# Own places for the gate weights of the fourth expert pair, and another order at the end of the routing

## What is computed

```python
gp = jax.nn.softmax(x @ w_group_router + b_group_router); g_val, g_idx = lax.top_k(gp, 1)
el_sel = (x @ w_expert_router + b_expert_router) # the 8 experts of that group
e_val, e_idx = lax.top_k(jax.nn.softmax(el_sel), 2); e_val = e_val / e_val.sum()
combine = one_hot(g_idx * 8 + e_idx) * (g_val * e_val)
for e in range(32):
    hdn = jax.nn.silu(x @ w_gate[e]) * (x @ w_up[e])        # 1024 -> 256
    y = y + combine[:, e:e + 1] * (hdn @ w_down[e])         # 256 -> 1024
```

## Time and profile before

| | us |
|---|---|
| median of 3 runs | 614.64 (614.0 to 615.8) |
| the profiled execution | 614.34 |
| its span | 612.7 |
| TensorE busy | 532.0 (87%) |
| VectorE busy | 218.6 (36%) |
| ScalarE busy | 169.6 (28%) |
| GpSimd busy | 139.4 (23%) |
| all transfers | 140.80 MB, mean 230 GB/s |

### The profile page before, as it was taken

How to read it: one execution, slowest core, us unless ns; L and a number is a source line. 1 busy time by engine, 2 the same in 40 slices (tenths; PEclk the granted TensorE clock), 3 DMA queues, 4 the chain that set the end, 5 groups by cost and what they waited for, 6 DMA issues and landing times.

```text
span 612.7 us, 9450 instructions
## 1 busy us (share of the span) xinstructions
PE 532.0 (87%) x3252; PEld 391.5 (64%) x3253; DVE 218.6 (36%) x602; ACT 169.6 (28%) x421; POOL 139.4 (23%) x230
## 2 busy tenths in 40 slices
PE   4899999999989999999956976899938779999984
PEld 4788988987558668888854633566624555556651
DVE  4753244333667755347671121111101111121111
ACT  6833343332443332135431111111111111111110
POOL 0132232222503200015525012122201122222212
PEclk9999999999999999999966999999959989999998
DMA  8741000012313101299894299999999999999993
GB/s 315 294 108 36 13 23 1 24 46 76 116 57 104 34 35 36 60 409 420 317 355 190 95 318 376 371 374 395 378 375 404 372 382 387 375 358 370 383 339 71
DMA packets 33445, 140.80 MB, mean 230 GB/s; under 512 B 10488, under 2 KB 11147, under 8 KB 21350
## 3 DMA queue, kind: packets, MB, share of 16 engines
q1 hardware_dynamic: 25776, 124.33, 52.4%
q0 software_dynamic: 5856, 12.60, 8.5%
q10 hardware_dynamic: 1766, 3.25, 1.6%
HBM read 131.15 MB, written 16.46 MB: 241 GB/s over the span
## 4 chain that ended last, share of the span: by engine, by line
DMA 26%; PE 22%; DVE 4%; issue 3%; ACT 1%; POOL 1%; DVEq 0%; POOLq 0%; ACTq 0%; SPq 0%
PE ps L847 11%; DMA expert_w<-in_w_gate 11%; DMA expert_w<-in_w_up 9%; PE ps L863 5%; DMA token_gates<-gate_rows 2%; DMA more_rows<-token_rows,idx_now 2%; DMA g_rows<-token_rows,idx_all 1%; DMA token_rows<-h_sb 1%; PE ps L506 1%; PE ps L507 1%; PE ps L511 1%; PE ps L765 1%; DVE xT L1490 1%; PE ps L834 1%; ACT s_act L1134 1%
## 5 line engine op out<-in xcount | busy, mean ns | idle before, releaser
L847 PE MATMUL ps<-expert_w,xT 128*64 128x256 f32 x1152 | 134.1, 390 | 12.9 <-issue 5.1
L847 PEld LDWEIGHTS ps<-expert_w,xT 128*64 128x64 f32 x1152 | 98.6, 141 | 52.1 <-issue 22.2
L863 PE MATMUL ps<-expert_w,hT 128*64 128x512 f32 x272 | 63.9, 611 | 18.0 <-DVE hT L1508 16.8
L1664 POOL DMA_INDIRECT out<-y_sb,idx_now x17 | 27.2, 1602 | 175.9 <-issue 128.2
L1501 DVE SCALAR_TENSOR_TENSOR hid<-s_act,gate,ps 128x256 f32<-128x256 f32 x18 | 12.0, 666 | 139.5 <-ACT s_act L1134 139.5
L863 PEld LDWEIGHTS ps<-expert_w,hT 128*64 128x64 f32 x272 | 21.9, 140 | 49.2 <-issue 42.9
L1134 ACT ACTIVATE s_act<-ps,gate 128x256 f32<-128x256 f32 x18 | 8.5, 474 | 131.2 <-PE ps L847 131.2
L506 PE MATMUL ps<-w_in_hi,aT_hi 128*128 128x384 f32 (+2 forms) x120 | 43.7, 369 | 0.0
L507 PE MATMUL ps<-w_in_lo,aT_hi 128*128 128x384 f32 (+2 forms) x120 | 40.8, 345 | 0.0
L1513 DVE COPY y_sb<-ps 128x512 f32<-128x512 f32 x18 | 12.4, 692 | 74.1 <-PE ps L863 68.4
L1139 ACT ACTIVATE y_sb<-ps 128x512 f32<-128x512 f32 x18 | 10.8, 597 | 78.8 <-PE ps L863 73.2
(11 more groups left out here) (227 smaller groups left out, 924.6 us busy)
## 6 DMA issues: line engine op xcount, KB each, us to landing
expert_w<-in_w_gate SPq DMA_DIRECT2D x32, 1024.0 KB, 9.2
expert_w<-in_w_up SPq DMA_DIRECT2D x32, 1024.0 KB, 9.5
expert_w<-in_w_down SPq DMA_DIRECT2D x30, 1024.0 KB, 9.5
w_in_raw<-in_w_in SPq DMA_DIRECT2D x8, 608.0 KB, 10.4
w_out_raw<-in_w_out SPq DMA_DIRECT2D x8, 512.0 KB, 3.8
token_rows<-h_sb ACTq DMA_DIRECT2D x6, 512.0 KB, 8.3
out<-h_sb SPq DMA_DIRECT2D x6, 512.0 KB, 11.5
x_sb<-in_x_prompt SPq DMA_DIRECT2D x4, 512.0 KB, 12.7
```

The source lines that it names most:

```text
L847: mm = pe.matmul(ps[r, GU_BANK[q.o], g * FH:(g + 1) * FH], xT[:, q.o, k, r], w_gu(b, lane, k, g), start=(k == 0), stop=(k == KD - 1))
L863: mm = pe.matmul(ps[r, 4 + half, :], hT[:, q.o, k, r], w_dn(b, lane, k, half), start=(k == 0), stop=(k == 1))
L1664: pool.indirect_dma_start(out=out, out_offset=bass.IndirectOffsetOnAxis(ap=idx, axis=0), in_=y_sb[:, buf, :], in_offset=None, compute_op=A ...
```

## The change

- The gate parts of pair 3 get places of their own, w_gate3_0 behind w2 and w_gate3_1 at the end of the third region. To make room, `more_rows` becomes the fourth buffer of y_sb, which the surplus pass uses for its results.
- SyncE loads parts 0 to 3 of pair 2, waits for the first gather, loads parts 4 and 5, then waits for the surplus slot products, the stored token weights and all indices, and loads the gate parts of pair 3. The refill of pair 3 then has only the up and down parts.
- The loops of all engines write out pairs 0 to 3 and 13 to 15 and run three turns over pairs 4 to 12.
- TensorE's order at the end of the routing becomes: logits of tile 5 (first half), transposes, slots(1), ranks(4), slots(2), slots(3), logits (second half), slots(4), more_slots(1) to (3), ranks(5), the token column of slots(5) alone, the two other columns of slots(5), the count product, more_slots(4), more_slots(5).
- VectorE computes the weight factors of tile 5 after the token indices of the first gather instead of ahead of `slot_of`.

Nothing is put into TensorE's pauses beyond this work.

```diff
-        (qT, w_in_raw, aT_hi, cT_kv, q_x, w_in_lo, o_hi, o_lo, w_out_hi_o, w_out_lo_o, w2) = region(
+        (qT, w_in_raw, aT_hi, cT_kv, q_x, w_in_lo, o_hi, o_lo, w_out_hi_o, w_out_lo_o, w2, w_gate3_0) = region(
-            [("expert_w2", [P, 2, 3, 2 * D], F32)], pick="under_")
+            [("expert_w2", [P, 2, 3, 2 * D], F32), ("w_gate3_0", [P, 2 * D], F32)], pick="under_")
...
-            [("g_rows", [P, 3, D], F32), ("more_rows", [P, D], F32), ("xT", [P, 2, KD, P], F32), ("y_sb", [P, 4, D], F32),
-             ("s_act", [P, 2, FH], F32), ("hid", [P, 2, 2, P], F32), ("hT", [P, 2, 2, P], F32), ("more_gate", [P, PAIRS, 2], F32)],
+            [("g_rows", [P, 3, D], F32), ("xT", [P, 2, KD, P], F32), ("y_sb", [P, 4, D], F32),
+             ("s_act", [P, 2, FH], F32), ("hid", [P, 2, 2, P], F32), ("hT", [P, 2, 2, P], F32), ("more_gate", [P, PAIRS, 2], F32),
+             ("w_gate3_1", [P, 2 * D], F32)],
             pick="under_")
         weights = (w0, w1, w2)
+        w_gate3 = (w_gate3_0, w_gate3_1)
+        more_rows = y_sb[:, 3, :]
...
-        def w_gu(b, lane, k, g):
-
+        def w_gu(j, b, lane, k, g):
+            if isinstance(j, int) and j == 3 and g == 0:
+                return w_gate3[lane][:, k * FH:(k + 1) * FH]
             return weights[b][:, lane, g, k * FH:(k + 1) * FH]
...
-                sp.dma_start(weights[b][:, lane, what, :], src).then_inc(part_in[n], 16)
+                first = isinstance(j, int) and j == 3 and what == 0
+                sp.dma_start(w_gate3[lane][:, :] if first else weights[b][:, lane, what, :], src).then_inc(part_in[n], 16)
...
-            for b in range(3):
-                pair(b, 0, b, False)
-            with eng.Fori(1, PAIRS // 3) as i:
-                for b in range(3):
-                    pair(3 * i + b, i, b, False)
-            pair(PAIRS - 1, PAIRS // 3, 0, True)
+            for j in range(4):
+                pair(j, j // 3, j % 3, False)
+            with eng.Fori(1, 4) as i:
+                for b in range(1, 4):
+                    pair(3 * i + b, i + b // 3, b % 3, False)
+            for j in range(PAIRS - 3, PAIRS):
+                pair(j, j // 3, j % 3, j == PAIRS - 1)
...
-            load_pair(sp, 2, 2)
+            load_pair(sp, 2, 2, range(4))
+            sp.wait_ge(main.gathered[0], 16)
+            load_pair(sp, 2, 2, range(4, 6))
+            sp.wait_ge(more_mm, NT)
+            sp.wait_ge(gates_stored, 16 * NT)
+            sp.wait_ge(idx_done, 13)
+            load_pair(sp, 3, 0, range(2))
...
-                used(lambda q: q.g_mm)
-                load_pair(sp, j, b, range(2))
+                if not (isinstance(j, int) and j == 3):
+                    used(lambda q: q.g_mm)
+                    load_pair(sp, j, b, range(2))
                 used(lambda q: q.gu_mm)
                 load_pair(sp, j, b, range(2, 4))
                 used(lambda q: q.y_mm)
-                if isinstance(j, int):
+                if isinstance(j, int) and j == PAIRS - 1:
                     load_last_down(j, b)
                 else:
                     load_pair(sp, j, b, range(4, 6))
 
-            with sp.Fori(1, PAIRS // 3) as i:
-                for b in range(3):
-                    refill(3 * i + b, b)
-            refill(PAIRS - 1, 0)
+            refill(3, 0)
+            with sp.Fori(1, 4) as i:
+                for b in range(1, 4):
+                    refill(3 * i + b, b % 3)
+            for j in range(PAIRS - 3, PAIRS):
+                refill(j, j % 3)
...
+            def slot_product(i, at, block, cols, last):
+
+                for c in range(2):
+                    mm = pe.matmul(ps[:, 5, at + cols.start * E:at + cols.stop * E], slot_a[:, i % SLOT_BUFS, 2 * block + c, :],
+                                   slot_b[:, i % SLOT_BUFS, c, cols, :].rearrange("t n e -> t (n e)"),
+                                   start=(i == 0 and block == 0 and c == 0), stop=(last and c == 1), skip_group_check=True)
+                return mm
+
             def slots(i):
 
                 pe.wait_ge(slot_a_done, 2 * i + 1)
                 pe.wait_ge(slot_b_done, 2 * (i + 1))
-                for c in range(2):
-                    mm = pe.matmul(ps[:, 5, 0:3 * E], slot_a[:, i % SLOT_BUFS, c, :], slot_b[:, i % SLOT_BUFS, c, :, :].rearrange("t n e -> t (n e)"),
-                                   start=(i == 0 and c == 0), stop=(i == NT - 1 and c == 1), skip_group_check=True)
-                mm.then_inc(slot_mm, 1)
+                slot_product(i, 0, 0, slice(0, 3), False).then_inc(slot_mm, 1)
+
+            def last_slots():
+
+                pe.wait_ge(slot_a_done, 2 * NT - 1)
+                pe.wait_ge(slot_b_done, 2 * NT - 1)
+                slot_product(NT - 1, 0, 0, slice(0, 1), False).then_inc(slot_mm, 1)
+                pe.wait_ge(idx_done, 2)
+                pe.wait_ge(slot_b_done, 2 * NT)
+                slot_product(NT - 1, 0, 0, slice(1, 3), True).then_inc(slot_mm, 1)
 
             def more_slots(i):
 
                 pe.wait_ge(slot_a_done, 2 * (i + 1))
-                if i == 1:
-                    pe.wait_ge(idx_done, 5)
-                for c in range(2):
-                    mm = pe.matmul(ps[:, 5, 128:128 + 3 * E], slot_a[:, i % SLOT_BUFS, 2 + c, :], slot_b[:, i % SLOT_BUFS, c, :, :].rearrange("t n e -> t (n e)"),
-                                   start=False, stop=(i == NT - 1 and c == 1), skip_group_check=True)
-                mm.then_inc(more_mm, 1)
+                slot_product(i, 128, 1, slice(0, 3), i == NT - 1).then_inc(more_mm, 1)
...
             h_transposes(last, 1)
+            slots(1)
+            ranks(last - 1)
+            slots(2)
+            slots(3)
             logits(last, 1)
-            ranks(last - 1)
-            for i in range(1, last):
-                slots(i)
+            slots(last - 1)
+            for i in range(1, last - 1):
+                more_slots(i)
             ranks(last)
-            slots(last)
+            last_slots()
             pe.wait_ge(pos_done, NT)
             pe.matmul(ps[:, 6, 128:128 + E], ones_bf, m_sum[:, 0, :], start=True, stop=True).then_inc(total_mm, 1)
-            for i in range(1, NT):
-                more_slots(i)
+            pe.wait_ge(idx_done, 5)
+            more_slots(last - 1)
+            more_slots(last)
...
             route_experts(NT - 1)
-            route_weights(NT - 1)
             slot_of(NT - 1)
             dve.wait_ge(slot_mm, NT)
 
@@ -1457,7 +1485,9 @@
                                     ).then_inc(idx_done, 1)
 
             slot_tokens(0, idx_all)
+            route_weights(NT - 1)
             table_place(NT - 1)
+            dve.wait_ge(slot_mm, NT + 1)
             slot_factors(0, gate_all)
```

More of the change, by code:

```diff
@@ L153, in build @@
          w_uq_lo, h_sb, x_res, w_out_raw, w_out_hi_p0, a2T, h_junk, slot_a, slot_b, route_f, route_u, r_bias,
-         g_rows, more_rows, xT, y_sb, s_act, hid, hT, more_gate) = region(
+         g_rows, xT, y_sb, s_act, hid, hT, more_gate, w_gate3_1) = region(
             52224,
@@ L835, in gather_transposes, with gate_up @@
                 mm.then_inc(q.x_tr, 1)
-            def gate_up(q, b, n):
+            def gate_up(q, b, n, j):
                 pe.wait_ge(q.x_act, n + 1)
@@ L846, in gate_up @@
                             r = slice(lane * LANE, (lane + 1) * LANE)
-                            mm = pe.matmul(ps[r, GU_BANK[q.o], g * FH:(g + 1) * FH], xT[:, q.o, k, r], w_gu(b, lane, k, g),
+                            mm = pe.matmul(ps[r, GU_BANK[q.o], g * FH:(g + 1) * FH], xT[:, q.o, k, r], w_gu(j, b, lane, k, g),
                                            start=(k == 0), stop=(k == KD - 1))
@@ L881, in pair @@
             def pair(j, i, b, last):
-                gate_up(main, b, j)
+                gate_up(main, b, j, j)
                 def opening(n):
-                    gather_transposes(over, more_rows[:, :], over.gathered[0], n + 1)
-                    gate_up(over, b, n)
+                    gather_transposes(over, more_rows, over.gathered[0], n + 1)
+                    gate_up(over, b, n, j)
                 def closing(n):
@@ L1683, in more_gather @@
                 ready((over_idx_in, 32 * (m + 1)))
-                gather(more_rows[:, :], table, idx_now[:, 6:7], over.gathered[0])
+                gather(more_rows, table, idx_now[:, 6:7], over.gathered[0])
                 gather(more_gate[:, :, :].rearrange("t j n -> t (j n)"), gate_table, idx_now[:, 6:7], more_gate_in)
```

## The result

| | median us | runs |
|---|---|---|
| before | 614.32 | 4 (613.38 to 615.8) |
| after | 638.58 | 4 (630.97 to 644.74) |

The ratio is 1.0351, with a 95% interval from 1.0257 to 1.0445: slower by 3.5%, where 611.0 us and a range up to 615.0 were forecast. The profiled execution of after is the fastest of its four, 630.97 us with a span of 629.2. That is 16.6 us above the profiled execution of before, while the medians lie 24.3 us apart; what the trace shows accounts for the 16.6, and the other 7.7 us are not traced.

A forecast was written before the change was run, and what follows sets the result against it. TensorE and the weight transfers were taken to tie, both hanging on the first gather. Gains 1.3 + 4.0, less 0.2 and 1.7, gave 3.4 us: 610.9 from the profiled 614.34, forecast 611.0 us, range 606.5 to 615.0 (8 in 10).

The forecast's parts named there:

- Longer straight code: TensorE's pair loop: two more written-out pairs stall on fresh code, 0.85 us each, 1.7 us lost (0 to 6.5).
- slower rival: Last three written-out pairs: each stalls 3.26 us on code blocks, 9.8 us in all, giving 619.0 us; chance 9%.
- Down parts after the gather: SyncE's pair 2 down loads, issued after the first gather: gather lands in 4.8 us, gain 4.0 us (0 to 5.3).
- Tail of the routing: New TensorE and VectorE order at the routing's end: first gather issued 1.3 us earlier (0.3 to 2.0).
- ScalarE next: Copy of first transposed rows: ScalarE free between 325.0 and 326.6, on average 0.2 us late, 3 us at worst.
- Own places: Gate parts of pair 3, loaded early into their own places: costed at 0, since the queue behind had run dry.
- Bytes did not count: Rival on the weight stream: if it alone bound from 348 us, 2 MB would save 5.0 us, giving 606.0; chance 7%.
- Both chains tie: Expert loop's end: TensorE and weight transfers finish together, TensorE waiting only 0.25 us for weights before the last up product.
- 5.1 us of stalls: TensorE in pairs 1 and 2: unexplained stalls of 1.80 and 3.26 us, spread over six fresh-code pairs, 0.85 each.

The follow-up runs named there:

- after_minus17: Changed kernel with eight transposes (16 instructions) left out of never-run code in pair 0, loop in seven blocks: 614.25 us, ratio 0.9982 to before.
- late_only: Kernel before with only the down parts of pair 2 moved after the first gather: 610.8 us, ratio 0.9914.
- start_only: Kernel before with the new order at the routing's end and late down parts of pair 2, no own places or written-out pairs: 611.47 us, ratio 0.9927.
- lean_before: Kernel before with the never-run code of further surplus passes left out of TensorE's program: 612.29 us, ratio 0.996.
- before_plus256: Kernel before with 256 never-run instructions (one block) added in pair 0: 618.95 us, ratio 1.0059.

## Why the prediction was wrong, point by point

- **The step that failed is "Longer straight code".** It put the risk into the two new written-out pairs, 0.85 us each, 1.7 in all with 0 to 6.5 as bounds. What it missed is the loop between them, whose fetching it put at nothing. It used "none from 478 to 590 where the loop repeats" as the price of a loop and did not ask on what that zero rested: the loop of before fitted with a margin of 54 instructions, and the change moved it by 573. In place of the 1.7 us the trace of after has 24.3 us more of stalls: 8.5 to 9.4 us at each of the two returns to the loop's head, 1.15 to 1.66 us in each third pair, and 2.74 us at the first pair behind the loop. The shifted kernels show the cause: 60 instructions make the kernel before 30 us slower, 16 fewer make the change 24 us faster.
- The cost of the written-out pairs alone was within its bounds: without the refetch (after_minus17) the stalls grow by some 2.8 us, forecast 1.7.
- The slower rival named the code blocks and the Trainium skill's rule on taken branches, but at the last three pairs and at 3.26 us each, 619.0 in all. The mechanism was near, the place and the price were not, and the range left it out. The preference for full unrolling that the Trainium skill states in the same section did not carry over to a part of the pairs here: writing out more of them pushed the rest over the limit.
- **Down parts after the gather**: forecast 4.0 us for the gather (4.8 to landing). Measured in after 6.0 from issue to transposes, 2.8 less than before; in late_only 4.75, 4.0 less. So the size holds where this is the only change, and it is all of the gain that the runs can tell: 3.5 us by the medians of late_only, 5.3 by its ratio.
- **Tail of the routing**: forecast 1.3 us earlier. In after the gather is issued 11.2 us after the last store of h instead of 13.2, so 2.0 us. But with the late down parts most of this is given back in the gather's longer landing (6.9 us in start_only against 4.75 in late_only): the two terms were added and are not independent. Sum forecast 5.3, measured 4.8.
- **ScalarE next**: forecast free between 325.0 and 326.6, on average 0.2 us late. Measured 327.5 with the layer ahead 1.8 us later, no loss.
- **Own places cost and bring nothing**: right, shown twice (0.02 us faster, 0.9 us slower). SyncE issues the down parts of pair 3 10.8 us after its up parts, as forecast, with the gap in the transfers at 356 to 360 us. Bytes did not count.
- **Both chains tie**: right for as long as the loop is not refetched. In after_minus17 TensorE waits for weights four times in the last pairs (1.80 and 2.05 us in the rows shown, 6.8 in all): what the start wins on TensorE's side meets the stream there.
- The 5.1 us of stalls in the earlier trace rows, which the forecast spread over all fresh code, hang on the code that is leapt over: they vanish without it (lean_before), and a longer leap costs more (before_plus256). Why pair 2 stalls 1.3 us in one kernel and 3.3 in another with the same leap stays open, and so does why pairs 3 to 5 of before, fetched for the first time and with the same leaps, do not stall at all.

## What to carry to other kernels

A hardware loop has a price that hangs on where it lies in the code: here 1705 instructions are free in seven blocks of 256 and cost some 10 us at each return to the loop's head in eight, so any edit ahead of a long loop can cost more than it brings. Count the instruction queue's packets before and after, and if they rise by more than the new code, shift or shorten the code before judging the edit; code that is never run costs too, by the leap over it. And load early only what a transfer would otherwise be late for: the useful part of this change was to load something later, out of the way of the gather on the path; late_only, little more than one wait of SyncE, stands at 0.9914 of before, the lowest of the complete kernels (start_only at 0.9927 is not told apart from it).

## What the runs showed of the hardware

- TensorE's instruction blocks are 256 instructions, with edges that stay at the same instruction count from kernel to kernel here (4034, 4546, 6850). The loop of 1705 or 1706 instructions is fetched once where it touches 7 blocks (q8: 28, 29, 35 and 36 packets, about one for each block of the program) and again at every turn where it touches 8 (53 and 56).
- Under a full stream of weights (339 to 397 GB/s during the five waits) the refetch at a return to the loop's head holds TensorE for 8.0 to 9.4 us. The trace shows it as "issue" or, once, under the name of a weight load that had landed at least 28 us before the wait began.
- A leap forward over code that is not run can stall TensorE: pair 0 leaps over some 190 instructions with 1.80 us of stall at pair 1, and with 256 more the stall is 8.44 us and the kernel 3.3 us slower. The same program stalled by nothing and by 2.69 us in two executions with other loads beside it.
- One indirect gather of 128 rows took 8.8 us from issue to landing beside 2 MB of fresh loads, 4.75 to its reader without them.
